# One folded sum for layer 1's norm, and unit 31 on the undivided input

## The reference, cut to what matters

```python
def rms_norm(x, g):
    return x * lax.rsqrt(jnp.mean(x * x, axis=-1, keepdims=True) + EPS) * g

def moba_layer(x, norm_g, w_in, q_norm_g, k_norm_g, w_out):      # layer 1
    h = rms_norm(x, norm_g)
    q, k, v, z = jnp.split(jnp.einsum('bsd,de->bse', h, w_in), 4, axis=-1)
    ...                                                          # per-head norms, attention -> o
    return jnp.einsum('bse,ed->bsd', o * jax.nn.silu(z), w_out)

def reference(x, ...):
    x = x + pool_conv_layer(x, ...)                              # layer 0
    return x + moba_layer(x, ...)
```

## Time and profile before

| | |
|---|---|
| median of 3 runs | 329.39 us (329.38 to 329.5) |
| the profiled execution | 329.37 us, its span 327.4 us |
| busy: TensorE | 321.8 us |
| busy: VectorE | 261.1 us |
| busy: ScalarE | 235.8 us |
| DMA | 64.79 MB |

### The profile page before, as it was taken

One profiled execution on the slowest core, in us unless ns is written; L12 is line 12 of the kernel. 1 busy time (PEld: TensorE's weight loads), 2 busy tenths in 40 slices (PEclk: granted clock), 3 DMA queues, 4 the chain that ended last, 5 costly groups with the idle time before them and its releaser, 6 DMA issues.

```text
span 327.4 us, 5849 instructions
## 1 busy us (share of the span) xinstructions
PE 321.8 (98%) x2244; PEld 295.5 (90%) x2244; DVE 261.1 (80%) x482; ACT 235.8 (72%) x436; POOL 51.2 (16%) x58
## 2 busy tenths in 40 slices
PE   8999999999999999998999999999999999999995
PEld 8899999999999999997999999988887777778885
DVE  2799989999999999999895898846556887758533
ACT  4687999997999889987766557814756667566630
POOL 0050024423224112120000000005500231400000
PEclk9999999999999999999999999999999999999999
DMA  7988478969999699984539244780635323200003
GB/s 275 413 278 355 156 265 224 203 148 344 346 328 214 122 411 292 217 270 93 249 143 397 104 148 152 279 322 13 243 130 166 132 103 129 114 2 0 2 0 130
DMA packets 12843, 64.79 MB, mean 198 GB/s; under 512 B 1424, under 2 KB 1552, under 8 KB 6544
## 3 DMA queue, kind: packets, MB, share of 16 engines
q1 hardware_dynamic: 8064, 53.78, 43.3%
q0 software_dynamic: 4608, 10.49, 17.7%
q10 hardware_dynamic: 144, 0.15, 0.2%
HBM read 52.88 MB, written 1.05 MB: 165 GB/s over the span
## 4 chain that ended last, share of the span: by engine, by line
PE 90%; ACT 4%; DVE 3%; issue 1%; POOL 0%; DVEq 0%; ACTq 0%; POOLq 0%
PE bank L1077 24%; PE bank L1078 23%; PE bank L1079 23%; PE bank L1111 4%; PE bank L1137 3%; PE bank L1185 2%; PE bank L1291 2%; PE bank L1318 2%; PE bank L1154 2%; PE bank L1145 2%; PE bank L1304 2%; ACT scratch L548 1%; DVE scratch L856 1%; ACT w_hi L461 1%; PE bank L1270 1%
## 5 line engine op out<-in xcount | busy, mean ns | idle before, releaser
L740 DVE TENSOR_TENSOR w_lo<-raw,w_hi 128x1024 fp32r<-128x1024 f32 x80 | 95.3, 1222 | 16.9 <-ACT w_hi L461 16.7
L461 ACT CAST w_hi<-raw 128x1024 fp32r<-128x1024 f32 x88 | 88.6, 1047 | 7.5 <-DMA raw<-w 3.8
L1077 PE MATMUL bank<-h_hi,w_hi 128*128 128x256 f32 x320 | 91.1, 285 | 0.0
L1079 PE MATMUL bank<-h_hi,w_lo 128*128 128x256 f32 x320 | 90.5, 283 | 0.0
L1078 PE MATMUL bank<-h_lo,w_hi 128*128 128x256 f32 x320 | 90.5, 283 | 0.0
L1078 PEld LDWEIGHTS bank<-h_lo,w_hi 128*128 128x128 f32 x320 | 61.4, 192 | 0.1
L1077 PEld LDWEIGHTS bank<-h_hi,w_hi 128*128 128x128 f32 x320 | 61.4, 192 | 0.1
L1079 PEld LDWEIGHTS bank<-h_hi,w_lo 128*128 128x128 f32 x320 | 61.4, 192 | 0.0
L856 DVE SCALAR_TENSOR_TENSOR scratch<-scratch,params 128x256 f32<-128x256 f32 x106 | 43.4, 482 | 0.2
L1077 PE MATMUL bank<-ya_hi,w_hi 128*128 128x256 f32 x144 | 42.6, 296 | 0.0
L1078 PE MATMUL bank<-ya_lo,w_hi 128*128 128x256 f32 x144 | 40.7, 282 | 0.0
(11 more groups left out here) (106 smaller groups left out, 522.2 us busy)
## 6 DMA issues: line engine op xcount, KB each, us to landing
raw<-w SPq DMA_DIRECT2D x49, 1024.0 KB, 6.9
side_v<-side_ring POOLq DMA_DIRECT2D x24, 256.0 KB, 6.5
w_lo<-raw POOLq DMA_DIRECT2D x8, 512.0 KB, 7.3
X<-xT SPq DMA_DIRECT2D x2, 512.0 KB, 5.2
out<-X SPq DMA_DIRECT2D x4, 256.0 KB, 2.6
consts<-const SPq DMA_DIRECT2D x1, 290.0 KB, 13.3
params<-vec ACTq DMA_DIRECT2D x1, 149.0 KB, 4.9
```

The lines of the kernel that those rows point to most:

```text
L461: nc.scalar.copy(halves(w_hi, cut_slot(n), half), halves(raw, n % RAW, half)).then_inc(hi_cut, 1)
L740: nc.vector.tensor_tensor(halves(w_lo, cut_slot(n), half), halves(raw, n % RAW, half), halves(w_hi, cut_slot(n), half).bitcast(F32), ALU.s ...
L1077: nc.tensor.matmul(dst, wh, ah, start=start, stop=False, skip_group_check=True)
L1079: return nc.tensor.matmul(dst, wl, ah, start=False, stop=stop, skip_group_check=True)
```

## The change

The folds are written in one table, and fold takes a part of it. For layer 1's norm VectorE makes two more folds, (0,6,2) and (0,1,1), ahead of the last low_h of the undivided input, so all squares are in tile 0. TensorE makes one sum over it, after k = 5 of unit 29 (SUM3_AT), in place of two blocks of two tiles. Unit 31 joins EARLY[1]: it reads ya_hi and ya_lo, VectorE scales its result (between cut_lo(33) and cut_lo(34)), and ScalarE's Silu of it waits for that. The wait for the divided input moves from unit 31 to unit 32. The other calls of fold (group 1) make the same four folds as before.

```diff
+SQUARE_FOLDS = (0, 2, 2, 2), (0, 4, 2, 3), (0, 6, 2, 4), (0, 1, 1, 4)
...
+SUM3_AT = 5
...
-EARLY = (BG[0],), (Z1[0], Z1[1])
+EARLY = (BG[0],), (Z1[0], Z1[1], Z1[2])
...
-            def fold(group, pairs):
+            def fold(group, first, last):
 
                 nonlocal folds
-                steps = ((0, 2, 2), (0, 4, 2), (0, 6, 2), (0, 1, 1)) if pairs == 4 else ((0, 2, 2), (0, 4, 2))
-                for i, (a, b, n) in enumerate(steps):
-                    if i < 3:
-                        dve.wait_ge(sq_ready, 4 * group + i + 2)
-                    if i:
+                for a, b, n, squares in SQUARE_FOLDS[first:last]:
+                    dve.wait_ge(sq_ready, 4 * group + squares)
+                    if first or (a, b) != SQUARE_FOLDS[first][:2]:
                         dve.wait_ge(folded, folds)
...
-            fold(1, 4)
+            fold(1, 0, 4)
...
+                if m == 4:
+                    fold(2, 2, 4)
                 if m:
                     low_h(1, m - 1)
                 if m == 2:
-                    fold(2, 3)
+                    fold(2, 0, 2)
...
-                    channel_step(n, k, {Z1[0]: 1, Z1[2]: 2}.get(n))
-                    if n == Z1[0] and k == 1:
-                        square_sums(6, (0, 1), bank[0], False)
-                    if n == Z1[0] and k == 2:
-                        square_sums(0, (6, 7), bank[0], True)
+                    channel_step(n, k, {Z1[0]: 1, Z1[3]: 2}.get(n))
+                    if n == Z1[0] and k == SUM3_AT:
+                        square_sums(8, (0,), bank[0], True)
```

## The result

The changed kernel takes 333.48 us (median of four executions, 333.47 to 333.74) against 329.5 before: ratio 1.012, 95% interval 1.0105 to 1.0135, slower. A fifth execution took 806.98 us and is left out of every number here; what disturbed it is not known. The profiled execution took 333.48 with a span of 331.6, so the span is 4.2 us longer than before.

What follows compares the result with a forecast made beforehand. The prediction took TensorE as the bound, waiting for nobody there; -1.29 us (sums) and +3.7 (wait for unit 34's low half) gave +2.4, so 331.8 us, with some 0.8 for 331.2 to 333.5.

Steps and rivals of the forecast that it cites:

- the clock's case: Rival: TensorE's clock falls in the gap before units 33/34, costing 1.7 us more: 333.5, range 332.3 to 334.5; chance 0.21.
- The summed case: Whole kernel: the forecast as summed, 331.8 us, own range 331.3 to 332.3; chance 0.70.
- TensorE's work, -1.29 us: Layer 1's norm sums on TensorE: four go, one comes, 1.29 us less; without a wait units 33/34 begin at 207.93.
- The folds, 0.61: VectorE's two new folds ahead of the last low_h: the cut of unit 30 and what follows start 0.61 us later.
- No wait in units 29 to 32: TensorE in units 29 to 32: it doesn't wait for the shifted VectorE work; margins of 0.37 to 0.8 in unit 29.
- The wait of about 0.6 for h_lo: Start of unit 31: the divided input would have brought a wait of about 0.6 us; reading ya_hi avoids it.
- The place in the queues: Unit 34's low cut, behind unit 31's scaling and gate: 2.22 us later by queue place, 2.83 with the folds.
- the sum of +2.4: Whole kernel: -1.29 from the sums plus a 3.7 us TensorE wait for unit 34's low half makes +2.4 us.
- The likeliest case: Whole kernel: the forecast as summed, +2.4 us to 331.8 us, without a clock fall; chance 0.70.
- The bound of 2.7: Clock rival: upper limit of the loss, 0 to 2.7 us, from a low-clock stretch of up to 5.4 us.
- The later sum: Rival: the single sum after unit 29's k = 5 delays root and reciprocal: 332.5 or so; chance 0.02.
- the case of 328.1: Rival: the queues don't bind before units 33/34, leaving only the 1.29 us gain: 328.1; chance of faster 0.04.

Runs made afterwards that it cites:

- experiment 11: The changed kernel run once more, unaltered, for more executions with the full idle stretch: median 334.36 us, ratio 1.0139.
- experiment 4: The changed kernel with the first halves of units 33 and 34 cut ahead of the scalings and gates: 328.16 us, ratio 0.9962.
- experiment 1: The changed kernel without the late scaling, unit 31 reading the divided input again; single folded sum kept: 329.75 us, ratio 1.0008.
- experiment 6: The changed kernel with the order of experiment 4, but unit 31 on the divided input as in experiment 1: 328.89 us, ratio 0.9983.
- experiment 2: The late scaling of unit 31 alone, with the two blocks of sums and two folds of the kernel before: 331.2 us, ratio 1.0055.
- experiment 3: The changed kernel with 14 unread matmuls of the ones matrix between unit 32 and the first 512-wide matmul: 331.77 us, ratio 1.0075.
- experiment 5: The changed kernel with unit 34's high cut ahead of unit 31's gate and its low cut ahead of unit 31's scaling: 329.93 us, ratio 1.0009.
- the second set: The later executions of the unaltered changed kernel, made as experiment 11: median 334.36 us, ratio 1.0139.

## Why the prediction was right in its range and wrong in its likeliest case

**The range.** The measured 333.48 lies in the range of 331.2 to 333.5 by 0.02 us. That is luck: the edge was drawn through the middle of the clock's case, and the same kernel in experiment 11 has a median of 334.36, outside it. The summed case's own range, 331.3 to 332.3, was missed.

**TensorE's work, -1.29 us.** Right. With nothing in its way (experiment 4) the change gives 329.57 - 328.16 = 1.4 by the medians and 1.27 by the profiles, where 1.29 was forecast. The first matmul of the pair starts 23.46 us after unit 29, the place forecast (207.93 - 184.49 = 23.44). L1157, the line of the sums now, has the 20 records that were said.

**The folds, 0.61.** Right: the cut of unit 30 starts at 188.68 in place of 188.03, in a profile that is 0.03 later there, and experiment 1, without the late scaling, has the same 0.61 at unit 34's cut. At the end of the chain, the cast of unit 34 was forecast at 209.21 and began at 209.25, its low cut at 210.28 and 210.31.

**No wait in units 29 to 32.** Right; the waits of the changed kernel name none of TensorE there. The wait of about 0.6 for h_lo which the late scaling was said to avoid shows in experiments 1 and 6 as 0.6.

**The place in the queues, and the sum of +2.4.** Right, and shown apart by when unit 34's first low cut begins: 2.23 later with the late scaling alone (experiment 2; 2.22 was forecast), 0.61 later with the folds and without the late scaling (experiment 1), and 2.84 with both (2.83 was forecast). With the clock kept up the whole is 331.77 us against the 331.8 of the sum (experiment 3), and the pair starts 2.43 later. Experiment 4 removes the wait by order alone, without touching the work; experiment 5 shortens it to 1.2 us.

**The likeliest case.** Wrong. The step that failed is the weighing of the clock: "a gap that is hardly longer needn't trip it in every execution, while the time is a median", with 0.21 for it. At the gap of this kernel all eight executions fell. What misled was the one fall in the trace of before: I took its 3.2 us of rest as about the length that is needed, and a gap of 3.5 to 3.7 as on the edge. The counts show that 3.2 is no edge: a third of the executions fell with 2.4 us of rest, and the level can come down when TensorE is at work again. The rule that the Trainium skill gives (TensorE: Matmul & The Clock Gate, What's actually happening), idleness halves the clock and work lifts it, agrees with the trace, which has 0.50 behind the gap and 1.00 from 216.48.

**The price of the clock.** The 1.7 us of that case was chosen inside 0 to 2.7, not worked out, so that it came out (333.5; by the profiles 115.89 - 114.18 = 1.7) for five of the eight executions is luck. The bound of 2.7 was too low: it took the slow records at the start of the kernel, 5.4 us, as the longest low stretch, and the long stretch of the second set took 6.8 us and cost 3.0. That the records of the earlier trace rows ran at half speed fits experiment 3, whose records of the same kind took 0.118 us against 0.223. But the granted clock of before reads 1.00 over that stretch, so there the column doesn't show it (columns as in the earlier trace rows):

```profile
0.00:5.00 5.00, 4.02 (x19) 4.03 (x20) 0.00 (x0) 1.49 (x2) 0.76 (x9) 1.00 0.59 168
```

**The other rivals.** The later sum didn't bind: the reciprocal began at 190.95, behind VectorE's cut, as forecast. The queues bound, so the case of 328.1 didn't come; it is the time of the kernel with the order mended (328.16).

## What to carry to other kernels

When a multiplication or a wait is added in a hand-written order, don't price its duration but follow what stands behind it on both engines: 0.68 us of scaling moved a weight cut by 2.2 us, because it closed a loop from VectorE to ScalarE and back. Work taken off the bounding engine is worth something only as far as its next inputs are early; here unit 34's first low half had 0.4 us of slack (ready at 208.82 for 209.22), and the 1.29 came through only when the first halves were made first. And price an idle stretch of TensorE at more than its length: here 2.4 us of it cost 1.7 us more in a third of the executions, and 3.5 us cost 1.7 or 3.0 more in all eight. Filling it with matmuls that nobody reads won the 1.7 back (experiment 3); mending the order took away gap and loss and let the gain of the sums through (experiment 4).

## What the runs showed of the hardware that I had not expected

The granted clock came down more often the longer the idle time was (none in 20 executions at 1.7 us or less, 3 of 9 at 2.4, 7 of 10 at 3.1, 8 of 8 at 3.5), and the low stretch had two lengths. In the first profile it began 5.2 us after the last matmul ahead of the gap had started, with TensorE at work again for 1.4 us, and lasted 3.41 us. In the second it began 3.2 us after that matmul, still in the gap, and lasted 6.8 us, from 211.25 to 218.07. The latter gives 334.3 to 334.8 us in place of 333.5. What decides between the two was not tried; the first set of the changed kernel had only the short one, the second mostly the long one.
